# A two-layer hybrid decoder trunk: weight splits of the mixer moved and halved, feed-forward transposes taken in pairs

## The reference

```
x = x + 0.5 * rmsnorm(swiglu(rmsnorm(x, ffn1_pre_g), w_gate, w_up, w_down), ffn1_post_g)
x = x + rmsnorm(hybrid_mixer(rmsnorm(x, mix_pre_g), ...), mix_post_g)
x = x + rmsnorm(memory_cross_attn(rmsnorm(x, xa_pre_g), rmsnorm(mem, xa_mem_g), ...), xa_post_g)
x = x + 0.5 * rmsnorm(swiglu(rmsnorm(x, ffn2_pre_g), w_gate, w_up, w_down), ffn2_post_g)
```

## Time and profile before

| | |
|---|---|
| three runs | 1229.1, 1230.49, 1231.89 us; median 1230.49 |
| the profiled execution | 1229.08 us, its span 1227.3 us |
| PE busy | 98% of the span |
| DVE, ACT, POOL busy | 65%, 55%, 13% |
| DMA | 179 GB/s, queue of the weights 52.7% of 16 engines |
| mean granted clock of PE | 0.998 |

### The profile page before, as it was taken

The page is one execution under the profiler, slowest core; times in us unless marked ns, Lnnn a source line. Parts: engine busy times, 40 slices in busy tenths (PEclk is TensorE's granted clock), DMA queues, the critical chain, the costliest instruction groups (busy, mean ns, idle before and its releaser), DMA issues.

```text
span 1227.3 us, 19448 instructions
## 1 busy us (share of the span) xinstructions
PE 1205.5 (98%) x6120; PEld 1008.2 (82%) x6120; DVE 799.4 (65%) x1214; ACT 671.1 (55%) x1117; POOL 158.7 (13%) x282
## 2 busy tenths in 40 slices
PE   6999999999999999999999999999999999999997
PEld 5888888779898888888888888887799988888886
DVE  6776645778556577665476665477866557676655
ACT  6555545566555565553475544367566445555544
POOL 1000002663100100000010000036432001000001
PEclk9999999999999999999999999999999999999999
DMA  8555565453554355555465555563535435555563
GB/s 337 184 193 192 180 206 172 171 178 108 181 177 144 131 191 186 178 208 194 158 208 177 198 192 189 187 213 129 164 128 191 152 125 168 182 195 175 197 208 127
DMA packets 32916, 220.06 MB, mean 179 GB/s; under 512 B 4272, under 2 KB 4528, under 8 KB 8768
## 3 DMA queue, kind: packets, MB, share of 16 engines
q1 hardware_dynamic: 32544, 218.98, 52.7%
q10 hardware_dynamic: 288, 0.02, 0.0%
HBM read 217.93 MB, written 1.05 MB: 178 GB/s over the span
## 4 chain that ended last, share of the span: by engine, by line
PE 94%; DVE 2%; issue 2%; POOL 1%; DMA 1%; ACT 1%; DVEq 0%; SPq 0%; ACTq 0%; POOLq 0%
PE acc L469 29%; PE acc L471 28%; PE acc L470 28%; PE tb L530 4%; DVE w_lo L1183 1%; PE acc L779 1%; PE mb L763 1%; PE mb L621 1%; DMA raw<-in_gu 1%; PE mb L714 0%; PE mb L698 0%; ACT w_hi L872 0%; DVE w_lo L1177 0%; PE mb L683 0%; PE mb L658 0%
## 5 line engine op out<-in xcount | busy, mean ns | idle before, releaser
L1183 DVE SCALAR_TENSOR_TENSOR w_lo<-raw,gains,w_hi 128x512 fp32r<-128x512 f32 x580 | 415.9, 778 | 50.1 <-ACT w_hi L872 49.3
L469 PE MATMUL acc<-w_hi,xT_hi 128*128 128x512 f32 x1024 | 409.8, 400 | 4.9 <-DVE w_lo L1565 4.0
L872 ACT ACTIVATE w_hi<-raw,gains 128x512 fp32r<-128x512 f32 x580 | 370.2, 714 | 61.0 <-PE acc L471 60.8
L471 PE MATMUL acc<-w_hi,xT_lo 128*128 128x512 f32 x1024 | 401.3, 392 | 0.0
L470 PE MATMUL acc<-w_lo,xT_hi 128*128 128x512 f32 x1024 | 400.7, 391 | 0.0
L469 PEld LDWEIGHTS acc<-w_hi,xT_hi 128*128 128x128 f32 x1024 | 193.3, 189 | 47.8 <-DVE w_lo L1565 4.4
L471 PEld LDWEIGHTS acc<-w_hi,xT_lo 128*128 128x128 f32 x1024 | 193.2, 189 | 41.7
L470 PEld LDWEIGHTS acc<-w_lo,xT_hi 128*128 128x128 f32 x1024 | 193.4, 189 | 37.7
L1177 DVE TENSOR_TENSOR w_lo<-raw,w_hi 128x1024 fp32r<-128x1024 f32 x112 | 123.6, 1145 | 72.5 <-ACT w_hi L866 71.9
L937 ACT ACTIVATE th<-acc,r_half 128x256 f32<-128x256 f32 x88 | 41.7, 474 | 197.4 <-PE acc L471 197.0
L866 ACT ACTIVATE w_hi<-raw 128x1024 fp32r<-128x1024 f32 x112 | 105.4, 990 | 77.2 <-PE acc L471 77.2
(11 more groups left out here) (173 smaller groups left out, 1240.8 us busy)
## 6 DMA issues: line engine op xcount, KB each, us to landing
raw<-in_gu SPq DMA_DIRECT2D x92, 1024.0 KB, 5.2
raw<-in_down SPq DMA_DIRECT2D x32, 1024.0 KB, 5.1
raw<-in_in SPq DMA_DIRECT2D x24, 1024.0 KB, 5.2
raw<-in_kv SPq DMA_DIRECT2D x16, 1024.0 KB, 5.1
raw<-in_down SPq DMA_DIRECT2D x16, 768.0 KB, 4.2
raw<-in_out SPq DMA_DIRECT2D x8, 1024.0 KB, 5.1
raw<-in_q SPq DMA_DIRECT2D x8, 1024.0 KB, 5.2
raw<-in_o SPq DMA_DIRECT2D x8, 1024.0 KB, 5.2
```

What stands on the lines that cost most here:

```text
L469: pe.matmul(o, st_hi, mv_hi, start=first, stop=False)
L471: return pe.matmul(o, st_lo, mv_hi, start=False, stop=last)
L872: act.activation(w_hi[:, slot, k, :], raw[:, slot, k, :], ACT.Copy, scale=gains[:, ds(g, 1)]).then_inc(s_hi, 1)
L1183: dve.scalar_tensor_tensor(w_lo[:, slot, k, :], raw[:, slot, k, :], gains[:, ds(g, 1)], w_hi[:, slot, k, :].bitcast(F32), ALU.mult, ALU.su ...
```

## The change

Four edits:

1. Feed-forward, PE: for even j the transposes of chunks j-2 and j-1 stand together halfway through the first pass of chunk j; for odd j there are none, and the transposes of chunk 0 behind the first pair of chunks are gone. Those of chunk 10 stay where they were.
2. Feed-forward, ACT and DVE: `h_hi` and `h_lo` of j-2 and j-1 stand ahead of the first tanh or gated tile of an even chunk j.
3. Mixer, ACT: `split_after(5)` to `(8)` each stand ahead of a `project` or `exp_decay` that they stood behind, and `project(3, 0)` stands ahead of `exp_decay(4)`. Mixer, DVE: the same four halves are cut in two and laid around `level_out(0)` to `(5)`.
4. Mixer, POOL: each `mem_norm` one level later.

```diff
 # PE, feed-forward
                 def up(j, i=0):
+                    def two_before():
+                        h_transposes(l, f, j - 2, i)
+                        h_transposes(l, f, j - 1, i)
                     for t in range(TT):
-                        chunk_pass(l, c0 + j, q0 + j, t, xT_hi, xT_lo, x_ci=i * 4, x_q=i)
-                        if t == 0:
-                            h_transposes(l, f, j - 1, i)
+                        chunk_pass(l, c0 + j, q0 + j, t, xT_hi, xT_lo, x_ci=i * 4, x_q=i,
+                                   mid=two_before if t == 0 and j % 2 == 0 else None)
...
-                h_transposes(l, f, 0)
 # ACT, feed-forward
                 def up(j, i=None):
+                    if j % 2 == 0:
+                        h_hi(j - 2, i)
+                        h_hi(j - 1, i)
                     tanh(j, 0, i)
-                    h_hi(j - 1, i)
                     split_hi(l, c0 + j + 1, 1, i)
...
-                h_hi(0, None)
 # ACT, mixer
                 exp_decay(l, 2)
+                split_after(5)
                 exp_decay(l, 3)
                 project(2, 1, v_tok[:, 1, COL:2 * COL], r_8)
-                split_after(5)
+                split_after(6)
...
+                project(3, 0, v_tok[:, 0, 0:COL], r_pre)
                 exp_decay(l, 4)
-                project(3, 0, v_tok[:, 0, 0:COL], r_pre)
-                split_after(6)
+                split_after(7)
                 exp_decay(l, 5)
                 project(3, 1, v_tok[:, 1, 0:COL], r_pre)
-                split_after(7)
+                split_after(8)
                 exp_decay(l, 6)
-                split_after(8)
                 exp_decay(l, 7)
 # DVE, feed-forward
                 def up(j, i=None):
+                    if j % 2 == 0:
+                        h_lo(j - 2, i)
+                        h_lo(j - 1, i)
                     gated(j, 0, i)
-                    h_lo(j - 1, i)
...
-                h_lo(0, None)
 # DVE, mixer
                 retention_mask(1)
+                split_lo(l, C_IN + 4, 0, ks=(0, 1))
                 level_out(0)
-                split_after(5)
+                split_lo(l, C_IN + 4, 0, ks=(2, 3))
+                split_lo(l, C_IN + 4, 1, ks=(0, 1))
                 level_out(1)
-                split_after(6)
+                split_lo(l, C_IN + 4, 1, ks=(2, 3))
                 level_out(2)
-                split_after(7)
+                split_lo(l, C_IN + 5, 0, ks=(0, 1))
                 level_out(3)
-                split_after(8)
+                split_lo(l, C_IN + 5, 0, ks=(2, 3))
+                split_lo(l, C_IN + 5, 1, ks=(0, 1))
                 level_out(4)
+                split_lo(l, C_IN + 5, 1, ks=(2, 3))
                 level_out(5)
 # POOL, mixer
-                    if n in (3, 4):
-                        mem_norm(l, n - 3)
+                    if n in (4, 5):
+                        mem_norm(l, n - 4)
```

## The result

Six executions of the changed kernel took 1220.53 to 1221.5 us, median 1221.31; six of the kernel before 1229.1 to 1231.89, median 1230.03. The ratio is 0.9931, 95% interval 0.9920 to 0.9941: faster by 0.7%, or 8.7 us. The forecast was 1222.6, in a range of 1220.6 to 1227.0. The profiled execution took 1221.25 us, its span 1219.3.

What follows compares the result with a forecast made beforehand. PE is busy 98% of the span, so mainly its waits can be won: 6.3 us in the mixers plus 0.8 from joined transposes, 7.1 off 1229.08, gives 1222.0. Set between that and 1223.4, the forecast was 1222.6, range 1220.6 to 1227.0.

Steps and rivals of the forecast that it cites:

- the sum for the profiled execution: Whole kernel: 6.3 us from the mixer and 0.8 from the feed-forwards, 7.1 us off the profiled 1229.08, giving 1222.0.
- What holds level 4: Mixer: ACT's wait in `project(3, 1)` delays DVE's tiles, these the copy of level 3, so level 4 starts 1.98 us late.
- The copies' ends: Layer 0's mixer: copies of levels 3, 4, 5 done at 261.6, 266.6, 269.6, wanted at 263.66, 267.66, 271.66.
- The mixer's sum: Both layers' mixers lose 2.75 and 3.57 us, 4.7 in stalls and 1.6 in slow clock; 6.3 us to win.
- The joins: Feed-forwards: 20 joins of two groups of four transposes into one of eight, 0.04 us each, 0.8 us, between 0 and 1.4.
- a chunk with a group of four has 48 matmul spacings in 11.35 us: Feed-forward chunk: less 48 spacings of 0.2267 us, 10.88 in all, a group of four transposes costs 0.47 us.
- the sign given for it: Feed-forward: if right, two chunks take 22.66 instead of 22.70 us, eight transposes in a row, no idle time before them.
- The room at the new place: Halfway an even chunk's first pass: 0.96 us to spare; each us beyond costs 20; rival 1234.6 us, chance 0.03.
- The clock behind joined transposes: Rival, feed-forwards: PE's clock falls behind joined transposes, 1.6 us at each of 20 places, 1254.6 us; chance 0.02.
- From the profiled execution to the median: Profiled execution of before is 1.4 us under median 1230.49; gain gives 1222.0 or, from the median, 1223.4; 1222.6 chosen between.

Runs made afterwards that it cites:

- act_only: Changed kernel with DVE's and POOL's mixer lists set back to before, so in the mixer only ACT's order is new: median 1223.09 us, ratio 0.9941.
- early_k2: Changed kernel with the joined transposes after 6 of the first pass's 24 matmuls instead of after 12: 1226.12 us, one execution.
- early_k0: Changed kernel with the joined transposes ahead of the first pass's first matmul: 1252.79 us, one execution.
- pool_old: Changed kernel with POOL's two memory norms one level earlier, as in the kernel before: 1221.19 us, one execution.
- ffn_only: Kernel before with only the feed-forward edits 1 and 2, its mixer left as it was: median 1228.45 us, ratio 0.9987.

## Why the prediction was right

The forecast was 1.3 us too high: 0.7 in the sum for the profiled execution (7.1 forecast, 7.83 measured) and 0.6 that it had added between that execution and the median. The terms one by one:

- **What holds level 4** was right in each link: ACT's `project(3, 1)` ahead of the tiles, DVE's tiles ahead of the copy, the copy ahead of the level. `act_only` removes that stall by ACT's order alone. The copies' ends, forecast for 261.6, 266.6 and 269.6 us on the clock of the kernel before (0.42 less on that of the kernel after), came at 261.27, 265.99 and 269.23.
- **The mixer's sum** of 2.75 + 3.57 us measured 2.78 + 3.60. The part of it that is the clock's was read rightly for that trace, 1.6 us. That the profiled execution of before had exactly one such fall is chance, as the point on the median shows.
- **The joins** were the term that was mis-sized: 0.8 us forecast, 1.4 measured (4 x 0.35, or 0.07 for a join instead of 0.04). The step "a chunk with a group of four has 48 matmul spacings in 11.35 us" took one chunk for all, and one of the shortest: the mean of eight is 11.37, which makes a group of four 0.49 us instead of 0.47 and a join 0.07. Of the sign given for it, the 22.66 came (22.67), the 22.70 was 22.74. A difference that is multiplied by 20 should have been taken from a whole feed-forward.
- **The room at the new place** was put at 0.96 us; the four transposes that go ahead of the wait, which the prediction forgot, add to it. `early_k2` and `early_k0` bear out its price of 20 us for each us beyond.
- **The clock behind joined transposes**: the mean granted clock is 0.999, the windows of the kernel after show 1.00 in every stretch of 100 us up to 1200, and behind each of the 20 joined groups the matmuls keep their spacing of 0.227 us, which counts for more, since the windows also show 1.00 at the half-speed matmuls of the start. The Trainium skill (TensorE: Matmul & The Clock Gate, Part 4: PE-mode transpose) says that transposes don't count as TensorE activity in the way that matmuls do. These 20 places don't speak against that: eight in a row keep the 128x512 matmuls only 1.0 us apart, shorter than any stretch of the second table above, and longer rows weren't tried.
- **From the profiled execution to the median**: the profiled executions differ by 7.83 us, the medians by 8.72. The kernel before had a spread of 2.8 us in these runs, the kernel after 1.0. Falls by chance behind two waits, of 1.6 us or more each, would give such a spread and such a difference, and I had left half of it in the forecast. The mean granted clock of each timed execution bears this out: of 30 of the kernel before, 14 had a clock of 0.995 or 0.996 and took 1230.33 to 1231.84 us, 16 had 0.997 or 0.998 and took 1227.93 to 1229.89. The two groups don't overlap, so the spread goes with the clock; behind which waits it fell in the executions without a trace isn't shown.
- **One part of edit 3 without the other** I would have got wrong: for DVE's halves alone I expected most of the gain, and they gave none.

No version tried beat the kernel after; `pool_old` equals it.

## What to carry to other kernels

A copy that frees a bank for PE should have nothing ahead of it in its engine's list that waits for something later than the copy's own input; follow such a wait back through every list, since the one to mend may be two engines away, and check the moved step against the lists that haven't moved. Halve the work between two such copies only after what feeds it is early enough. Where PE is busy 98% of the time, a wait has a second price in the clock, so a stall of 2 us can be worth more than 2 us: here 1.6 us more in four of eight cases and 3.1 in a fifth.

## What the runs showed of the hardware

- PE's clock can fall to its lower level behind a wait of 1.8 to 2.0 us, in 9 of 28 cases, and did in 16 of 20 behind waits of 2.4 to 3.0; in none of 29 of up to 1.4 (the start of the kernel left out). A fall cost 1.6 us, and in one case (`ffn_only`, layer 0) 3.1. These runs don't separate the length of the wait from that of the whole stretch without 128x512 matmuls around it.
- Two groups of four 128x128 transposes cost 0.07 us more than one group of eight, wherever in the chunk they stand.
